# Routed experts: where the row-to-token table is laid out and loaded, when the first bias is picked, and which buffer the surplus block writes

## The reference, cut to what matters

```
logits = t @ w_router + b_router                     # t: 512 x 1024
top_val, top_idx = top_k(logits, 4)
probs = softmax(top_val)
# pairs (token, expert) sorted by expert, each expert's rows padded to blocks
def expert_block(xb, e):
    gu = xb @ w_gate_up[e] + b_gate_up[e]            # 1024 -> 2048
    g = minimum(gu[:, 0::2], 7); l = clip(gu[:, 1::2], -7, 7)
    return (g * sigmoid(1.702 * g) * (l + 1)) @ w_down[e] + b_down[e]
y = sum over k of probs[:, k] * row of pair (token, k)
x = x + gate * y, followed by a final norm
```

## Time and profile before

| | us |
|---|---|
| timed runs, median of 3 (lowest to highest) | 3504.11 (3500.72 to 3506.84) |
| profiled execution, its own time | 3497.2 |
| its span, first to last instruction | 3495.4 |
| TensorE matmul busy | 3028.8 (87%) |
| VectorE busy | 983.7 (28%) |
| ScalarE busy | 650.7 (19%) |
| GpSimd busy | 189.3 (5%) |
| mean granted TensorE clock | 0.917 |

### The profile page before, as it was taken

One profiled execution on the slowest core, in us unless ns is written; L12 is line 12 of the kernel. 1 busy time (PEld: TensorE's weight loads), 2 busy tenths in 40 slices (PEclk: granted clock), 3 DMA queues, 4 the chain that ended last, 5 costly groups with the idle time before them and its releaser, 6 DMA issues.

```text
span 3495.4 us, 45856 instructions
## 1 busy us (share of the span) xinstructions
PE 3028.8 (87%) x19729; PEld 1558.7 (45%) x19729; DVE 983.7 (28%) x1988; ACT 650.7 (19%) x1345; POOL 189.3 (5%) x179
## 2 busy tenths in 40 slices
PE   6898789999779998899889957398999998999873
PEld 3554334444345665666666643333333333333321
DVE  2344220000322212455545552211222211211114
ACT  1133000000003333343343430111011111011000
POOL 0000000000000000111111110100000000000001
PEclk9998889999889999999999958599999999999886
DMA  4135112112101115111110100747789899999994
GB/s 157 49 133 217 48 48 78 66 48 96 63 24 35 35 34 190 43 43 43 43 43 25 43 12 2 239 173 320 317 356 373 361 390 404 378 392 397 393 380 155
DMA packets 119373, 580.92 MB, mean 166 GB/s; under 512 B 12980, under 2 KB 24260, under 8 KB 72580
## 3 DMA queue, kind: packets, MB, share of 16 engines
q1 hardware_dynamic: 92464, 531.94, 38.7%
q10 hardware_dynamic: 20436, 24.26, 2.0%
q0 software_dynamic: 6272, 21.79, 1.7%
HBM read 549.48 MB, written 28.47 MB: 165 GB/s over the span
## 4 chain that ended last, share of the span: by engine, by line
PE 74%; DMA 12%; DVE 9%; ACT 2%; issue 1%; ACTq 1%; POOL 1%; SPq 0%; DVEq 0%; POOLq 0%
PE product_banks L829 37%; PE product_banks L1188 13%; DMA space<-in_wgu 10%; PE product_banks L1210 7%; PE score_banks L1091 3%; PE out_bank L956 1%; PE out_bank L876 1%; PE score_banks L893 1%; DMA y_rows<-zeros 1%; PE turn_bank L866 1%; PE out_bank L915 1%; DVE sq L1559 1%; PE score_banks L937 1%; DVE space L1780 1%; PE score_banks L934 1%
## 5 line engine op out<-in xcount | busy, mean ns | idle before, releaser
L829 PE MATMUL product_banks<-space 128*128 128x512 f32 (+2 forms) x4016 | 1437.2, 510 | 36.0 <-DVE space L1780 13.4
L829 PEld LDWEIGHTS product_banks<-space 128*128 128x128 f32 x4016 | 710.1, 195 | 646.3 <-issue 583.9
L1188 PE MATMUL product_banks<-space 128*32 128x512 f32 x5440 | 660.6, 620 | 112.5 <-DMA space<-in_wgu 86.5
L1188 PEld LDWEIGHTS product_banks<-space 128*32 128x32 f32 x5440 | 158.4, 111 | 487.7 <-issue 299.6
L1210 PE MATMUL product_banks<-space,rstd 128*32 128x256 f32 x5440 | 325.9, 394 | 1.1 <-ACT rstd L1499 0.6
L1903 DVE TENSOR_TENSOR sq<-product_banks,space 128x512 f32<-128x512 f32 x85 | 58.8, 692 | 820.0 <-PE product_banks L1188 820.0
L1301 ACT ACTIVATE space<-product_banks 128x512 f32<-128x512 f32 (+1 forms) x234 | 114.3, 525 | 854.7 <-PE product_banks L829 836.9
L1210 PEld LDWEIGHTS product_banks<-space,rstd 128*32 128x32 f32 x5440 | 182.9, 115 | 175.6 <-issue 78.8
L742 POOL TENSOR_TENSOR space<-space 128x512 f32<-128x512 f32 x112 | 132.2, 1194 | 1026.7 <-ACT space L1434 930.0
L1091 PE MATMUL score_banks<-space 128*128 128x64 f32 x896 | 132.9, 301 | 27.8 <-issue 21.1
L1091 PEld LDWEIGHTS score_banks<-space 128*128 128x128 f32 x896 | 129.5, 222 | 36.7 <-issue 32.5
(11 more groups left out here) (277 smaller groups left out, 2279.8 us busy)
## 6 DMA issues: line engine op xcount, KB each, us to landing
space<-in_wgu SPq DMA_DIRECT2D x256, 1024.0 KB, 15.5
space<-in_wdn SPq DMA_DIRECT2D x128, 1024.0 KB, 23.8
space<-in_wt SPq DMA_DIRECT2D x104, 1024.0 KB, 5.1
y_rows<-zeros ACTq DMA_DIRECT2D x2, 6400.0 KB, 29.3
y_rows<-zeros ACTq DMA_DIRECT2D x85, 128.0 KB
space<-in_wt SPq DMA_DIRECT2D x13, 512.0 KB, 4.5
space<-in_wt SPq DMA_DIRECT2D x4, 768.0 KB, 4.2
x<-in_xT SPq DMA_DIRECT2D x1, 2048.0 KB, 16.0
```

Of the source, the lines that this page charges most:

```text
L829: ins = nc.tensor.matmul(bank[0:rows, at:at + cols], lhsT, rhs, start=(i == 0), stop=(i == len(mm) - 1))
L1188: ins = nc.tensor.matmul(bank[ROWS * g:ROWS * g + ROWS, :], xT_[:, k, :], w[:, 512 * g:512 * g + 512], start=(k == 0), stop=(k == DC - 1))
```

## The change

The table in HBM gets another order for its first 2688 entries: row r is entered at (r mod 128) * 21 + floor(r / 128), so that partition p's 21 entries lie side by side. VectorE works this out in eight operations (`seat_no`, `destt`) ahead of the marks; the scatters use it, while the gathers of the output rows still use `desti`. GpSimd loads the table with one DMA of 128 runs of 84 bytes behind its scatters, and ScalarE no longer waits or loads. `pick(0)` stands right behind the marks, and the small product goes to a bank of its own, so it can lie beside the bias products. VectorE's wait for the cleared rows moves to block 1. Turn 1 is turned and copied at block 3 instead of block 1. The surplus block writes its rows into a buffer of its own (`cs`, a tensor that is free by then), VectorE's wait for the last two stores is gone, and TensorE and ScalarE handle the surplus block's inputs ahead of its bias.

```diff
+        destt = A.take(16)
+        seat_no = A.take(16)
...
+        yb_more = cs.rearrange("p a b -> p (a b)")
...
-            gp.wait_ge(s_dest, 1)
+            gp.wait_ge(s_at_row, 1)
...
-                    gp.indirect_dma_start(tokof, bass.IndirectOffsetOnAxis(desti_u[:, j:j + 1], 0),
+                    gp.indirect_dma_start(tokof, bass.IndirectOffsetOnAxis(destt_u[:, j:j + 1], 0),
...
-            gp.wait_ge(s_idx[0], 16)
+            gp.wait_ge(s_scat, 16 * TT * TOPK)
+            gp.dma_start(rows_of.bitcast(i32)[:, 0:N_TURNS], tokof[0:ROW_MORE, :].rearrange("(p n) o -> p (n o)", n=N_TURNS)).then_inc(s_idx, 16)
+            gp.wait_ge(s_idx, 16)
             for i in range(1, N_TURNS):
-                if i % 4 == 0:
-                    gp.wait_ge(s_idx[i // 4], 16)
...
-            nc.tensor.matmul(PT[:, 256:256 + N_MORE], more_col.broadcast_to([N_MORE, P]), ident[0:N_MORE, 0:N_MORE], start=True, stop=True).then_inc(s_mrow, 1)
+            nc.tensor.matmul(DN[1][:, 0:N_MORE], more_col.broadcast_to([N_MORE, P]), ident[0:N_MORE, 0:N_MORE], start=True, stop=True).then_inc(s_mrow, 1)
...
-                if j % 4 == 1 and j // 4 + 1 < N_TURNS:
+                if j % 4 == (1 if j >= 4 else 3) and j // 4 + 1 < N_TURNS:
                     turn_inputs(j // 4 + 1)
...
+                turn_inputs(b + N_TURNS)
                 expert_bias(b + N_FIXED)
-                turn_inputs(b + N_TURNS)
...
-            act.wait_ge(s_scat, 16 * TT * TOPK)
-            for c in range(len(s_idx)):
-                n = min(4, N_TURNS - 4 * c)
-                act.dma_start(rows_of.bitcast(i32)[:, 4 * c:4 * c + n],
-                              tokof[4 * P * c:4 * P * c + n * P, :].rearrange("(i p) o -> p (i o)", p=P),
-                              allow_slow_non_contiguous=True).then_inc(s_idx[c], 16)
...
+                act.wait_ge(s_up, n)
+                copy_inputs(b + N_TURNS, xTb[0])
                 act.wait_ge(s_y, n)
                 copy_bias(b + N_FIXED, biasb[0])
-                copy_inputs(b + N_TURNS, xTb[0])
...
-                store_rows(n, bass.ds(b * ROWS + ROW_MORE, ROWS), yb[0], s_ymore)
+                store_rows(n, bass.ds(b * ROWS + ROW_MORE, ROWS), yb_more, s_ymore)
...
-            V.tensor_copy(desti.bitcast(i32), destf).then_inc(s_dest, 1)
+            link(V.tensor_copy(desti.bitcast(i32), destf))
+            link(V.tensor_scalar(seat_no, destf, 1.0 / P, -(P - 1) / (2.0 * P), ALU.mult, ALU.add))
+            link(V.tensor_scalar(seat_no, seat_no, magic, None, ALU.add))
+            link(V.tensor_scalar(seat_no, seat_no, -magic, None, ALU.add))
+            link(V.tensor_scalar(seat_no, seat_no, float(1 - P * N_TURNS), None, ALU.mult))
+            link(V.scalar_tensor_tensor(seat_no, destf, float(N_TURNS - 1), seat_no, ALU.mult, ALU.add))
+            link(V.scalar_tensor_tensor(seat_no, destf, float(ROW_MORE), seat_no, ALU.is_lt, ALU.mult))
+            link(V.tensor_tensor(seat_no, seat_no, destf, ALU.add))
+            V.tensor_copy(destt.bitcast(i32), seat_no).then_inc(s_at_row, 1)
...
+            pick(0, four_e[:, 0:1])
             link(V.tensor_scalar(more_cmp, more_end[0:N_MORE, :], const("token_no")[0:N_MORE, 0:1], None, ALU.is_le))
             V.tensor_reduce(more_col, more_cmp, AX.X, ALU.add).then_inc(s_mcol, 1)
             dve.wait_ge(s_mrow, 1)
...
-            dve.wait_ge(s_ycleared, 32)
-            pick(0, four_e[:, 0:1])
             for j in range(N_FIXED_BLOCKS):
...
+                if j == 1:
+                    dve.wait_ge(s_ycleared, 32)
                 if j:
                     fixed_rows_out(j - 1)
...
-            for i in range(2):
-                dve.wait_ge(s_yst[i], 16 * ((N_FIXED_BLOCKS + 1 - i) // 2))
             V.memset(small[:, 9:10], 0.0).then_inc(s_ymore, 16)
...
-                rows_out(n, DN[0], biasb[0], yb[0])
+                rows_out(n, DN[0], biasb[0], yb_more)
```

More of the change, by code:

```diff
@@ L369, in build @@
         s_cnt = sem("expert_counts_ready")
-        s_dest = sem("rows_assigned")
         s_tab = sem("block_table_ready")
@@ L378, in build @@
         s_brow = sem("bias_rows_loaded")
-        s_idx = [sem(f"row_tokens_loaded{i}") for i in range(-(-N_TURNS // 4))]
+        s_idx = sem("row_tokens_loaded")
+        s_at_row = sem("table_rows_ready")
         s_tk = sem("more_tokens_loaded")
@@ L649, in build @@
         desti_u = desti.bitcast(mybir.dt.uint32)
+        destt_u = destt.bitcast(mybir.dt.uint32)
         block = ctx.enter_context(nc.Block())
@@ L1885, in _, with pick @@
             link(V.tensor_scalar(four_e, four_e, 4.0, None, ALU.mult))
+            def pick(n, col):
+                V.tensor_scalar(sel, const("group_of"), col, None, ALU.is_equal).then_inc(s_picks, 1)
+            pick(0, four_e[:, 0:1])
             link(V.tensor_scalar(more_cmp, more_end[0:N_MORE, :], const("token_no")[0:N_MORE, 0:1], None, ALU.is_le))
@@ L1888, in _ @@
             dve.wait_ge(s_mrow, 1)
-            link(V.tensor_scalar(four_more, PT[:, 256:256 + N_MORE], float(N_EXP - 1), None, ALU.min))
+            link(V.tensor_scalar(four_more, DN[1][:, 0:N_MORE], float(N_EXP - 1), None, ALU.min))
             link(V.tensor_copy(tab_i[0:1, 2 * N_EXP:2 * N_EXP + N_MORE], four_more[0:1, :]))
@@ L1896, in _ @@
                 link(V.tensor_scalar(prob[:, 4 * i:4 * i + 4], prob[:, 4 * i:4 * i + 4], small[:, 152 + i:153 + i], None, ALU.mult))
-            def pick(n, col):
-                V.tensor_scalar(sel, const("group_of"), col, None, ALU.is_equal).then_inc(s_picks, 1)
             def gated(n, bank, bias, to):
```

## The result

| | before | changed |
|---|---|---|
| median of the timed runs, us (lowest to highest) | 3503.86 (3500.72 to 3506.84, 4 runs) | 3449.44 (3448.03 to 3455.13, 4 runs) |
| profiled execution, its own time, us | 3497.2 | 3448.69 |
| its span, us | 3495.4 | 3446.6 |
| mean granted TensorE clock | 0.917 | 0.922 |

The changed kernel takes 0.9848 of the time before (95% interval 0.9831 to 0.9865). Both gains are where they were forecast. The head is larger than its term, the tail smaller.

A forecast was written before the change was run, and what follows sets the result against it. Bound at the head by ScalarE's scatter wait and six table loads, at the tail by VectorE's store wait. Head 26.4 (with part 1's 1.8 inside) plus tail 15.1 gives 41.5 us off the median 3504.11: forecast 3463, range 3455 to 3475.

The forecast's parts named there:

- D: Time block 0 starts earlier, 26.4 us; also a rival (0.05): something unseen holds the surplus block, tail gain absent, 3478.
- C: Rival, 0.05: weights, not products, pace the expert stage and absorb the head gain; only the tail is left, 3489.
- F: Rival, 0.03: block 0 still waits for the same moment and the surplus block for its store, 3504.
- E: Rival, 0.03: TensorE, rested less, gets its lower clock through the first expert's blocks 0 to 5, 3527.
- part 1: Seat numbers: eight more VectorE operations delay picks and scatters by 1.8 us; the scatters themselves don't change.
- A: Rival, 0.10: scatter traffic may hold the picks' results up to the landing at 2247.4; head gain 19.5, 3470.
- Part 2: Head: ScalarE freed of wait and six issues, bias following the picks at once; block 0's up products end 26.4 us earlier.
- Part 3: Turn 1: GpSimd's load takes 10 us, rows come at 2266.4, hidden ahead of block 3; moving the turning costs zero.
- B: Rival, 0.08: GpSimd's load takes 23.8 us, so rows are late at block 3 and cost 7.2 us, 3470.
- Part 4: Tail: surplus block's own row buffer removes the store wait; the last down tile then bounds; gain 15.1 us.
- Rival G: Chance 0.01: at the head, weight transfers made ScalarE's 21.9 us and hold GpSimd's load too; head gain 7, 3482.

The follow-up runs named there:

- e11: The changed kernel unaltered, third time, as control on its chip: 3464.71 us, ratio 0.9903.
- first pair: The profiled kernel before (3503.86 us) and changed kernel (3449.44 us), ratio 0.9848.
- group 4: One chip: changed kernel a fourth time (3455.20 us), without scatters (3456.41), with sixteen further scatters (3453.78) or sixteen plain stores instead (3453.07).
- group 2: One chip: changed kernel again (3461.67 us), e6, e7, and the changed kernel with first bias ahead of picks and four row buffers (3462.73).
- group 3: One chip: e11, e12, and the changed kernel with weight loads (3466.27 us) or scatters (3466.43) held until the picks.
- e1: Changed kernel with scatters to the old addresses, table still loaded as 128 runs of 84 bytes: 3459.05 us, ratio 0.9855.
- e12: The kernel before, unaltered, a single execution: 3507.06 us.
- e3: The kernel before with only the tail's edits for the surplus block: 3489.93 us, ratio 0.9947.
- e2: The kernel before with the eight seat operations and scatters to the new addresses: 3498.60 us, ratio 0.9972.
- e4: The changed kernel with turn 1 turned at block 1 again: 3478.02 us, ratio 0.9917.
- e6: The changed kernel with the table's old order and one GpSimd load of 2688 pieces of 4 bytes: 3461.47 us, ratio 0.9860.
- e7: The changed kernel with the table's old order, entries 64 bytes apart, one strided load: 3462.78 us, ratio 0.9872.

## Why the prediction missed

**What bounds, and whether the gain survives:** right. ScalarE's queue was the bound, and a start D earlier moves everything behind block 5 by D (36.2 at block 0, 36.5 at the last gate/up wait), so C and F fell. The lower clock of E stayed away.

**The step that failed** is the end of the picks, in two sentences: "I take 2238.7 as the true end of the picks", and in part 1 "to other addresses of the same table; no change". The first made a number of one execution, the 5.5 us behind 2232.8, into a constant of the kernel. It is the price of the condition with gaps, and there it is no property of the picks but 2.8 us behind GpSimd's last scatter issue. Where it holds, the forecast of the head is close: signal forecast at 2240.5, in e11 (M within 0.3 us of before) at 2240.55; D forecast 26.4, in e11 2277.6 - 2250.6 = 27.0. Where it does not, the signal comes at 2232.9, 7.6 us earlier, the bias and up products run at the full clock, and the body is 7 to 12 us shorter (1101.6 and 1104.2 against 1111.0 and 1114.1). D was 9.8 above its term, within 0.1: 7.6 by the signal, 1.7 by the bias (up products 1.2 us behind the signal, not 2.9), 0.6 by the up products (7.2 us, not 7.8). I had noticed the gap and gave it a rival (A) on one side only, longer; the other side, that it is absent, had no chance at all.

The medians say this less sharply. Against the runs of the kernel before beside them, the changed kernel gained 54.4 us in the first pair and 54.4 in group 4, 47.2 in group 2 and 35.4 in group 3. So the medians of groups 2 and 3, 3461.67 and 3464.71, stand near the 3463 forecast in part by luck: neither gain is the 41.5.

**The second sentence** is needed too. With early signals and the old addresses the body is 1112.4 (e1), as long as with late signals: the down tiles are late then. The prediction saw 4.4 us to spare for these tiles (2257.8 against 2262.2), but 2262.2 is the end of block 0's down products; they begin 3.5 us earlier, so it was 0.9. My lower bound from the weights, 2245.7 by the earlier trace rows, was also read under the slow traffic; in the changed kernel the same tile landed at 2214.1 + 21.4 = 2235.5 at the latest:
```profile
L699 SPq DMA_DIRECT2D space<-in_wgu x2: 332/332/333, 2213.6 to 2214.1; - x2
...
DMA to landing us min/median/max: 19.5/20.4/21.4
```
So the 10 us need both, early signals and spread addresses. Only in the kernel before do the addresses pay by themselves, 6 to 11 us by body (against e12, before and e3), 8.7 by medians (e2).

**Part 2** was otherwise right: the bias follows the picks at once. **Part 3** was right in its sum. The load landed in 5.4 us (10 taken, B expected up to 23.8), the gather in 9.7 (8.7), the rows at 2259.2 against 2266.4, 3.7 us ahead of their use where 6.6 were forecast. Turn 1 at block 3 was costed at nothing, and e4 shows the price of the cover: 22.9. **Part 4:** 14.7 for 15.1, and D fell, but the bound was not the one forecast. The last down tile, landing 18.0 us behind block 83's rows (19.8 forecast), held nothing. The down products began at 15.8, as the working without tiles has it (14.3 to 16.3), and the lower clock made them 5.35 us long. That the sum came out is luck. The 2.4 us that the stretches ahead of it and behind it grew had no term.

**Rival G** had something in it. ScalarE's issues became 7 us shorter in e2, where the weights had got ahead while the scatters ran, so part of the 21.9 was the transfers'. But the head did not lose it: GpSimd's one issue took 0.58 us with the weights in flight at 421 GB/s, and 1.46 us as 2688 pieces of 4 bytes (e6). The rule of the Trainium skill, "DMA: Bandwidth & Descriptors", section "Issuing engines are not separate DMA queues", is that another issuing engine saves only the sequencer's time, which it calls usually small; by it the head would have gained 7. The 36.5 here disagrees.

**From the profiled execution to the median** is the second step that failed. The forecast took 41.5 from the median, as if both kernels' profiled executions stood equally far below their medians. The one before stood 6.9 below, the changed one 0.8. By profiled executions the forecast was 3455.7 and 3448.69 was measured, 7.0 less (10.1 more at the head, 2.8 less at the tail). By medians it was 3463 and 3449.44; 6.2 of these 13.6 us are this step and 0.4 is rounding. Without this step, or without the 10.1 us at the head, the median would have lain in the range of 3455 to 3475. The profiled execution before began the stage at M = 2213.7, e12 at 2225.5, which is room enough for the 6 us; it says nothing of the change.

## What to carry to other kernels

An idle time that nothing in the trace explains is a range, not a constant: price it at zero as well, above all where the change puts it on the path, and count whether the trace has all its events there. Before taking a landing time as a bound, ask which traffic it was read under and whether the change touches that. Scattering small entries to neighbouring addresses while weights stream in costs the weights; spread them. And run the kernel at more than one time before a difference of 10 us is put down to an edit.

## What the runs showed of the hardware

- Scatters of 4-byte entries that lie side by side held weight transfers at 192, 205 and 186 GB/s in three windows of 5 us of the kernel before and 205 and 257 in e1; with entries 84 bytes apart (the changed kernel) it was 412 and 413, with 64 bytes apart (e7) 410. The DMA engines' share was 0.86 or more in all of them. The Trainium skill, "DMA: Bandwidth & Descriptors", section "Specifications", says that pieces below 512 bytes are done as read-modify-write. All of these are pieces of 4 bytes, so that rule would slow both orders alike. The traces show that the distance counts as well.
- TensorE can stand for 0.2 to 4.5 us at a time while scatters are in flight, with nothing shown that it waits for, in all traces of one group and in none of another on the same chip. In the changed kernel ScalarE and VectorE then get its signals 7.5 us later (M + 26.5 against 19.0). In seven such traces that is 2.6 to 2.8 us after GpSimd's last scatter issue, and in all nine with gaps 107 to 196 of the scatters' 256 landing events are missing.
- Six strided loads of single 4-byte entries held ScalarE's queue for 21.1 to 22.0 us beside the weights (before, e3, e12). One load of all 2688 entries by GpSimd held its queue for 1.46 us and landed after 9.2 (e6), and as 128 runs of 84 bytes for 0.58 and 5.4.
- The same code before the router ended anywhere within 12.5 us from one execution to the next.
